# A float32 decoder step on one core: the MLPs' normed chunks, loading, latents, attention filling and final norm reordered

## The reference, cut to what matters

```python
def rmsnorm(x, g):
    y = x * rsqrt(mean(x * x, axis=-1) + EPS)
    return y * g

# layer 0: windowed attention and retention; layer 1: latent attention; a gated MLP after each
x = x + mixer_ab(rmsnorm(x, g_mix[0]))          # first norm: on the rows of x as they are loaded
x = x + conv_ffn(rmsnorm(x, g_ffn[0]))
x = x + mixer_c(rmsnorm(x, g_mix[1]))           # cq = rms(h @ w_dq), c, k_rope = h @ w_dkv, ...
x = x + conv_ffn(rmsnorm(x, g_ffn[1]))
y_prompt, y_sample = rmsnorm(x, g_final)        # the final norm, rows out
# conv_ffn: act = silu(conv3(h @ w_gate)) * (h @ w_value); act @ w_down,  D_FF = 2816
# mixer_c, per head: q = rope(cq @ w_uq), k = c @ w_uk and the rotary key, softmax, p @ v
```

## Time and profile before

| | |
|---|---|
| median of 3 runs | 3236.02 us (3235.65 to 3238.68) |
| profiled execution, its own time | 3237.81 us |
| its span, first instruction to last event | 3236.3 us |
| mean granted TensorE clock | 0.965 of full speed |
| PE busy | 3000.4 us, 93% |
| DVE, ACT, POOL busy | 1430.1, 834.2, 305.5 us |
| loading: first scaled block to last | 16.35 to 54.35 us |
| first MLP: first normed chunk, first product with a DVE `lo` in the third tile | 784.11, 813.23 us |
| latents: block begins, first product | 1578.56, 1604.17 us |
| latent attention, one pair with filling | 99.0 us, PE busy 88.66 |
| end of the last down product, end of span | 3207.47, 3236.3 us |

### The profile page before, as it was taken

How to read it: one execution, slowest core, us unless ns; L and a number is a source line. 1 busy time by engine, 2 the same in 40 slices (tenths; PEclk the granted TensorE clock), 3 DMA queues, 4 the chain that set the end, 5 groups by cost and what they waited for, 6 DMA issues and landing times. The chain is left out here.

```text
span 3236.3 us, 49732 instructions
## 1 busy us (share of the span) xinstructions
PE 3000.4 (93%) x20246; PEld 2711.9 (84%) x20246; DVE 1430.1 (44%) x2746; ACT 834.2 (26%) x1543; POOL 305.5 (9%) x280
## 2 busy tenths in 40 slices
PE   5999999889999999999598999889898999999997
PEld 4888899679999999999464665666698999999997
DVE  3334444444544444444413334433426444444445
ACT  3434311332221211121222222233323112121113
POOL 3101122003000000000200000033021000000002
PEclk7999999899999999999798999999899999999998
DMA  5112111751888411120301000066321112111101
GB/s 171 47 59 61 39 48 44 267 215 53 298 286 309 143 39 39 39 64 1 129 1 45 14 1 1 1 248 260 111 66 53 39 39 63 41 52 39 39 27 56
DMA packets 202540, 287.01 MB, mean 89 GB/s; under 512 B 12730, under 2 KB 174356, under 8 KB 194772
## 3 DMA queue, kind: packets, MB, share of 16 engines
q1 hardware_dynamic: 193944, 176.01, 17.0%
q0 software_dynamic: 8448, 108.93, 9.2%
HBM read 263.42 MB, written 88.40 MB: 109 GB/s over the span
## 5 line engine op out<-in xcount | busy, mean ns | idle before, releaser
L826 PE MATMUL psum<-mlp_halves,w_up 128*128 128x352 f32 x6336 | 1019.6, 323 | 17.8 <-DVE mlp_halves L544 14.4
L826 PEld LDWEIGHTS psum<-mlp_halves,w_up 128*128 128x128 f32 x6336 | 1014.1, 189 | 21.0 <-DVE mlp_halves L544 16.2
L864 PE MATMUL psum<-acts,w_down 128*128 128x352 f32 x3168 | 516.4, 323 | 7.8 <-DVE xT L1007 6.4
L864 PEld LDWEIGHTS psum<-acts,w_down 128*128 128x128 f32 x3168 | 510.4, 189 | 10.4 <-DVE xT L1007 7.6
L1007 DVE TENSOR_TENSOR xT<-xT,psum 128x352 f32<-128x352 f32 x528 | 274.6, 521 | 238.5 <-PE psum L864 238.5
L1290 PE MATMUL psum<-h_ab,w_in_halves 128*128 128x352 f32 x2016 | 341.8, 326 | 8.7 <-POOL w_in_halves L1590 7.6
L1290 PEld LDWEIGHTS psum<-h_ab,w_in_halves 128*128 128x128 f32 x2016 | 323.0, 189 | 22.5 <-issue 10.9
L913 ACT CAST acts<-window 128x1056 fp32r<-128x1056 f32 x44 | 47.4, 1076 | 708.2 <-PE psum L864 572.3
L491 POOL TENSOR_TENSOR norm_temps<-norm_temps 128x352 f32<-128x352 f32 x72 | 76.4, 1074 | 1429.4 <-ACT norm_temps L482 1426.6
L626 PE MATMUL psum<-mlp_halves,project_w 128*128 128x352 f32 x1152 | 188.0, 326 | 13.6 <-DVE project_w L654 13.6
L626 PEld LDWEIGHTS psum<-mlp_halves,project_w 128*128 128x128 f32 x1152 | 186.7, 191 | 14.3 <-DVE project_w L654 13.9
(11 more groups left out here) (317 smaller groups left out, 3341.8 us busy)
## 6 DMA issues: line engine op xcount, KB each, us to landing
mlp_raw<-in_w_up SPq DMA_DIRECT2D x88, 512.0 KB, 5.1
out_new_a_k_s<-in_cache_a_k POOLq DMA_DIRECT2D x8, 4088.0 KB, 15.3
out_new_a_v_s<-in_cache_a_v POOLq DMA_DIRECT2D x8, 4088.0 KB, 15.3
mlp_raw<-in_w_down SPq DMA_DIRECT2D x22, 1024.0 KB, 6.6
w_in_raw<-in_w_in_ab SPq DMA_DIRECT2D x28, 512.0 KB, 4.6
xT<-x_spill SPq DMA_DIRECT2D x2, 4224.0 KB, 16.8
ws_k_rows<-in_cache_a_k SPq DMA_DIRECT2D x8, 1024.0 KB, 10.4
ws_v_rows<-in_cache_a_v SPq DMA_DIRECT2D x8, 1024.0 KB, 10.1
```

The costliest lines, as they stand in the source:

```text
L826: mm = nc.tensor.matmul(c.bank[TILES * part + n][:, 0:TILE], w_up[s][:, w, part, k, :], h[:, x, k, tokens_of(n)], start=k + w + x == 0, st ...
L864: mm = nc.tensor.matmul(c.bank[6 + t % 2][:, 0:TILE], w_down[:, w, s, o * P:(o + 1) * P], acts[s][:, x, tokens_of(n)], start=s + w + x == ...
```

## The change

Six things are changed, in the order of the program.

1. Loading: the ring `whole` has three blocks instead of two, at a place of its own, and ACT rounds block b - 2 behind block b's copies.
2. The MLPs' beginning: DVE makes the whole chunks 0 to 3, then `lo` 1, then two whole chunks and one `lo` in turn, instead of eight whole chunks and four `lo`.
3. Latents: `w_dq` and `w_dkv` get a place outside the stage and are loaded by SP at the end of the first MLP. The block of `apply_plain` is gone: DVE applies the norm in the main block, a token tile at a time, and PE waits for the chunks of a block. The other loads and `first_loads` are issued in the main block.
4. Latent attention: `TILE_KINDS` begins with the four "k", and each "rope" comes behind a "q". Buffers have other addresses.
5. Latent samples: SP loads the first projection weights of the second MLP when the merge's fourth PE mark is there, so that MLP is called with `begun=True`.
6. The end: no sums of squares by chunk. PE turns blocks of `xT` to rows inside the last down product (five of nine, behind tiles 8, 10, 16, 18 and 20) and the other four behind it. ACT squares a block of rows with an accumulated sum and takes the root, DVE inverts. Blocks 0 to 4 are scaled by ACT and multiplied by the gain by POOL, blocks 5 to 8 are finished by DVE in one instruction, and SP stores each from the MLP's stream. The gain is loaded as 128 equal rows (512 KB) behind the second MLP's last up weights. `store_outputs` is gone.

```diff
 load_inputs
+    WHOLES = 3
+    whole = c.at("x_whole", [P, WHOLES, KC, P], F32, 112640)
-            for b in range(BLOCKS + 1):
+            for b in range(BLOCKS + 2):
...
-                if b >= 1:
-                    n = rows_of(b - 1)
-                    act.wait_ge(gained, START + 2 * b)
-                    nc.scalar.copy(h[:, 0, :, (b - 1) * P:(b - 1) * P + n], whole[:, (b - 1) % 2, :, 0:n]).then_inc(rounded, 1)
+                if b >= 2:
+                    n = rows_of(b - 2)
+                    act.wait_ge(gained, START + 2 * (b - 1))
+                    nc.scalar.copy(h[:, 0, :, (b - 2) * P:(b - 2) * P + n], whole[:, (b - 2) % WHOLES, :, 0:n]).then_inc(rounded, 1)
...
-                if b >= 2:
-                    dve.wait_ge(split, START + b - 1)
+                if b >= WHOLES:
+                    dve.wait_ge(split, START + b - WHOLES + 1)
 Mlp, DVE
-                        split.make_whole(dve, n)
+                        for k in range(KC):
+                            split.make_whole(dve, n, k)
+                            if k >= 3 and k % 2 == 1:
+                                split.make_lo(dve, nc.vector, n, k - 2)
                         if n == 0:
                             project.add(dve, KC - 1, 2)
-                        split.make_lo(dve, nc.vector, n, 1)
+                        split.make_lo(dve, nc.vector, n, KC - 1)
 Mlp, SP
+                    if ahead:
+                        sp.wait_ge(self.up_ready, START + (self.chunk0 + FC) * TILES)
+                        ahead(sp)
...
+                    if final:
+                        final.store(sp)
 Mlp, PE, last down product
+                            if last and final:
+                                if t in final.TURN_AT:
+                                    if t == KC:
+                                        pe.wait_ge(self.tail_taken, START + FILLED * (call + 1))
+                                    final.turn(pe, final.TURN_AT[t], (self.added, START + (LAST_GROUP + group0) * OUTS))
...
+                    if final:
+                        for b in range(final.EARLY, BLOCKS):
+                            final.turn(pe, b, (self.added, START + (LAST_GROUP + group0) * OUTS))
 Mlp, ACT
+                    if final:
+                        for b in range(BLOCKS):
+                            final.take_root(act, b)
+                            if b == 1:
+                                final.move(act, 0)
+                                final.move(act, 1)
+                            if b in (3, 4):
+                                final.move(act, b - 1)
+                            if b == 4:
+                                final.move(act, 4)
 Mlp, DVE
+                    if final:
+                        for b in range(final.EARLY, BLOCKS):
+                            final.invert(dve, b)
+                            final.finish(dve, b)
+class FinalRows:
+    EARLY = 5
+    TURN_AT = {8: 0, 10: 1, 16: 2, 18: 3, 20: 4}
+    INVERT_AT = {11: 0, 13: 1, 19: 2, 21: 3, 23: 4}
...
+    def turn(self, pe, b, added):
+        pe.wait_ge(added[0], added[1] + KC * ((b * P + rows_of(b) - 1) // TILE + 1))
+        if 3 <= b < 3 + self.EARLY:
+            pe.wait_ge(self.moved, START + b - 2)
+        elif b >= 3 + self.EARLY:
+            pe.wait_ge(self.finished, START + b - 2 - self.EARLY)
+        for k in range(KC):
+            mm = nc.tensor.transpose(self.rows(b)[:, k * P:(k + 1) * P], c.xT[:, k, block_of(b)], c.ident[:])
...
+    def take_root(self, act, b):
+        act.wait_ge(self.turned, START + b + 1)
+        nc.scalar.activation(self.junk[0:rows_of(b), :], self.rows(b), ACT.Square, accum_out=self.of(self.total, b)).then_inc(self.squared, 1)
...
+    def move(self, act, b):
+        act.wait_ge(self.inverted, START + b + 1)
+        self.c.nc.scalar.mul(self.y[0:rows_of(b), b, :], self.rows(b), self.of(self.inverse, b)).then_inc(self.moved, 1)
...
+    def finish(self, dve, b):
+        self.c.nc.vector.scalar_tensor_tensor(self.y[0:rows_of(b), b, :], self.rows(b), self.of(self.inverse, b), self.g[0:rows_of(b), :],
+                                              ALU.mult, ALU.mult).then_inc(self.finished, 1)
...
 latents
-            sp.dma_start(w_dq[:], d["w_dq"][0].rearrange("(k p) n -> p k n", p=P)).then_inc(in_ready, 16)
...
-        norm.apply_plain(1, load)
...
-                pe.wait_ge(in_ready, START + 80)
+                pe.wait_ge(weights.w_in, START + 32)
+                pe.wait_ge(g_in, START + 32)
...
+                        pe.wait_ge(applied, START + KC * ((b * P + rows_of(b) - 1) // TILE + 1))
...
+                norm.apply_plain(0, 1, applied)
...
+                norm.apply_plain(1, 1, applied)
...
+                    if b == 2:
+                        norm.apply_plain(2, 1, applied)
 LatentAttention
-        TILE_KINDS = [kind for n in range(TILES) for kind in (("rope", 0, n), keys[n])] + keys[TILES:]
-        TILE_KINDS += [("q", e, n) for e in range(2) for n in range(TILES)] + [("v", 0, n) for n in range(4)]
+        TILE_KINDS = keys + [kind for n in range(TILES) for kind in (("q", 0, n), ("rope", 0, n))]
+        TILE_KINDS += [("q", 1, n) for n in range(TILES)] + [("v", 0, n) for n in range(4)]
 latent_samples
+                sp.wait_ge(merge_pe, START + 4)
+                project.early(sp, w_out)
```

More of the change, by code:

```diff
@@ L753, in rest_up, with __call__ @@
                                        ALU.subtract).then_inc(self.up_split, 1)
-    def __call__(self, layer, w_out, mix, gain, project, norm, restored, begun, beside=None):
+    def __call__(self, layer, w_out, mix, gain, project, norm, restored, begun, beside=None, ahead=None, final=None):
         self.prepare(layer)
@@ L952, in _ @@
                     for n in range(TILES):
-                        split.make_lo(pool, nc.gpsimd, n, 0)
+                        for k in range(0, KC, 2):
+                            split.make_lo(pool, nc.gpsimd, n, k)
                     pool.wait_ge(norm.inverted, START + (sums.call + 1) * TILES)
@@ L958, in _ @@
                         beside(pool)
-                    for n in range(TILES):
-                        for o in range(1, KC - 1):
-                            next_sums.gather(pool, o, n)
+                    if final:
+                        for b in range(final.EARLY):
+                            final.gain(pool, b)
+                    else:
+                        for n in range(TILES):
+                            for o in range(1, KC - 1):
+                                next_sums.gather(pool, o, n)
                 @block.vector
@@ L2046, in latents @@
     QC = C_Q // P
-    in_ready = c.sem("lat_in_ready")
+    w_dq, w_dkv = weights.w_dq, weights.w_dkv
+    g_in = c.sem("lat_g_in")
+    rope_in = c.sem("lat_rope_in")
+    applied = c.sem("lat_applied")
     g_ready = c.sem("lat_g_ready")
@@ L3092, in trunk @@
                     with c.stage():
-                        latents(c, norm, cqT, cT, krT, c_rows, kr, c_stored, attention)
+                        latents(c, norm, latent_weights, cqT, cT, krT, c_rows, kr, c_stored, attention)
                     with c.stage():
```

253 lines of the change are left out of this document (129 added, 124 removed).

## The result

The changed kernel takes 3135.09 us, the median of four runs (3134.13 to 3136.97), beside 3235.84 for the kernel before; the ratio is 0.9692, with a 95% interval of 0.9675 to 0.9709.

A forecast was written before the change was run, and what follows sets the result against it. PE, busy 93% of the span, bounds the kernel, with roughly 236 us idle where stages begin and end. Savings 13.6 + 6 + 21.7 + 22 + 4 + 15.7 = 83; 3237.8 - 83 - 1.8 = 3153 us, range 3138 to 3177.

The forecast's parts named there:

- the rivals: Whole kernel: waits moved in filled steps (3181 us, 0.10), latents half (3164, 0.08), port lock (3162, 0.07), slower (3255, 0.03).
- One sign: MLPs' beginnings: the first of three tiles would no longer have a stretch at granted clock 0.50.
- the clock's term in latent attention: Filled pairs: six half-clock stretches cost up to 1.7 us each, 10.2; a quarter counted as saved, 2.5.
- The part's upper bound, 30: Latent attention: 22 us saved, bounds 0 and 30, from PE's waits for rotated queries and `w_ukT` and from the clock.
- Loading: Loading before the mixer: blocks 3.1 us apart instead of about 5.26, 13.6 us saved, bounds 8 to 16.
- The rival in which POOL is held as much as DVE: DVE and POOL shut each other out: loading 3.5 us less, MLPs' beginnings 6 less, total 3162; chance 0.07.
- The latents: Latents' beginning: PE starts near 1582.5 instead of 1604.17, 21.7 us saved, bounds 15 to 23.5.
- The end: Final norm, partly inside the last down product: span ends at 3220.6, 15.7 us saved, bounds 10 and 18.
- The MLPs' beginnings: Both MLPs' heads: each `lo` comes earlier, 6 us saved, 4.3 and 1.7, bounds 0 and 12.
- The second MLP's weights: Second MLP's beginning: ACT's wait of 4.25 us for its first weights goes, 4 saved, bounds 1 and 5.

The follow-up runs named there:

- the experiment: The changed kernel with DVE making all eight whole chunks before its four subtractions again, in both MLPs: 3141.05 us.

## Why the prediction was wrong

The mechanisms were right, all six, in place and sign: each wait that was to go is gone or much shorter, and none of the rivals came. One sign failed: the first tile of the first MLP still has a half-clock stretch, 3.4 us from 768.2. What was wrong are sizes, nearly all in one direction.

**The step that failed** is the clock's term in latent attention: "PE's other waits there, for ACT's probabilities, 9.7 in sixteen, stay and may keep the clock where it is, so I count a quarter: 2.5." The 9.7 us stayed, to the tenth, and the clock is 1.00: 29.0 us where 22 were counted, shown by the order of tiles alone and again by putting it back. These 7 us are the largest part of the 18 by which the forecast missed. In the three filled pairs PE's busy time fell by 10.7 us, with nearly as many products; that is the term counted at 2.5. Its idle time fell by 18.3, where 19.5 were counted. In the kernel before already none of the sixteen waits, 1.3 us at most, had a half-clock stretch with it; all six stretches in attention came with waits of 1.9 to 2.2. The part's upper bound, 30, held the truth; the value within it was chosen without a row that spoke for it. The Trainium skill's page "TensorE: Matmul & The Clock Gate", section "A second HAM failure mode: psum-queue depth-cycling", tells of a kernel in which short, frequent pauses between groups of products made the clock swing. This case's trace does not agree for pauses of up to 1.3 us: with sixteen of them in the four pairs after, from 1692.3 to 2002.7 us, the clock is 1.00. For pauses of 1.9 to 2.3 us it agrees in part: six of nine in the pairs of before came with a half-clock stretch.

**The clock elsewhere** was at 0.50 for 231 us before and for 118 after, but it explains no miss at the latents or at the end. At the latents PE's first product came 6.8 us ahead of the end of a 41.0 us stretch; after the change it came 8.6 us ahead of the end of one of 17.1. At the program's end a stretch of 17.1 us became one of 5.5, which begins when PE has no more to do, and the prediction's sum for the end had no half clock in it.

**Loading**, 13.6 counted. From the first scale to the last 17.3 us are gone, and the first scale comes 0.8 later, so it is 16.5, over the part's bound of 16: a block takes 2.79, not 3.1. (0.8 was put down for the semaphores. With the same code the first scale scatters from 16.9 to 18.6 us, so their price is not shown.) The value was put in the middle because DVE's scale would often begin beside POOL's subtraction. It does each time, but late in it, and takes 0.89, so DVE is under ACT's 2.79. ACT itself was read as 2.90, from the start of its rounding to the end of its copy, but the next rounding begins 0.1 before that end; and a scale begun in a subtraction ends 0.55 behind it in both kernels, not 0.7. The rival in which POOL is held as much as DVE shows in part: POOL's subtraction is 2.51 instead of 2.36, and it costs nothing, since POOL has a block's time of 2.79.

**The latents**, 24.3 instead of 21.7: the gains' small loads were put at some 4 us to landing and PE began 1.6 behind the stage's start; their issues take 0.24 us each, where the first of them took 1.75 behind the two big loads.

**The end**, 18.7 instead of 15.7: the last down product with its turns is 27.8, not 28.7 (a turn adds 0.9 to it, not 1.0); from there to the last compute it is 8.9, not 9.4 (a square with its root 1.33 to 1.56, not 1.5 each); and the tail behind that is 3.2 instead of 4.8. Why the tail is shorter is not shown; with all nine blocks behind the down product it was 2.4.

**The MLPs' beginnings**, 6 counted: 4.6 from before to after, 3.5 by the experiment, and the half-clock stretches make the difference. **The second MLP's weights**, 4 counted, 4.1 by the profile and 4.2 by undoing it. The 2.9 us in the samples' stage are in no term and are scatter. Without them the changed kernel would be at 3138.0, the edge of the range, and of the five runs of its second measurement, 3137.15, one lies inside. So it is scatter that puts the time just outside the range; the 16 to 18 us between it and the forecast of 3153 are not scatter.

## What to carry to other kernels

A wait of TensorE has two prices, its own length and the half-clock stretch that may follow it; where the profile shows such a stretch behind a wait that goes, count both, and take a discount only where a row shows another cause of the same length. In a ring between engines look for the instruction whose place in one engine's stream puts two blocks in series, as ACT's rounding did, before adding buffers. At a stage's end idle work on any engine is on the path, as all five have to leave.

## What the hardware showed that was not expected

The granted clock fell to 0.50 with one of three equal waits of 1.94 us, and with six of nine waits of 1.9 to 2.3 us in the kernel before, the three without being the longest. It fell as well 3.0 us into a run of 32 narrow products without any wait. A small load's issue on SP's queue took 0.24 us where nothing was ahead of it and 1.59 to 1.75 right behind two loads of 1.6 and 1.3 MB; the two issues after that took 0.36 to 0.48.
